# Three products of a delta-rule recurrence in all four quadrants of TensorE, the second head carried across by VectorE, and a weight subtraction moved to GpSimd

## The reference

```python
def delta_rule_scan(r, w, k, v, a, b):          # 12 heads, 512 tokens
    def step(S, inp):
        r_t, w_t, k_t, v_t, a_t, b_t = inp
        sa = jnp.einsum('bhvk,bhk->bhv', S, a_t)
        S = (S * w_t[:, :, None, :] + sa[..., None] * b_t[:, :, None, :]
             + v_t[..., None] * k_t[:, :, None, :])
        return S, jnp.einsum('bhvk,bhk->bhv', S, r_t)
```

## Time and profile before

| | us |
|---|---|
| median of 3 runs (lowest, highest) | 1069.5 (1069.06, 1071.4) |
| profiled execution, its own time | 1070.18 |
| profiled execution, span of its instructions | 1068.4 |
| TensorE busy | 1039.6 |
| VectorE busy | 653.9 |
| ScalarE busy | 453.0 |
| GpSimd busy | 5.6 |

### The profile page before, as it was taken

One profiled execution on the slowest core, in us unless ns is written; L12 is line 12 of the kernel. 1 busy time (PEld: TensorE's weight loads), 2 busy tenths in 40 slices (PEclk: granted clock), 3 DMA queues, 4 the chain that ended last, 5 costly groups with the idle time before them and its releaser, 6 DMA issues.

```text
span 1068.4 us, 22579 instructions
## 1 busy us (share of the span) xinstructions
PE 1039.6 (97%) x9816; PEld 823.4 (77%) x9816; DVE 653.9 (61%) x1025; ACT 453.0 (42%) x732; POOL 5.6 (1%) x10
## 2 busy tenths in 40 slices
PE   7999999999999989999999999999999999999998
PEld 5777777676777777777777767787888888888887
DVE  4569999977466665868677667664443223444322
ACT  5455555686335533443535245344432112443111
POOL 0000000000000000000000000000000000000000
PEclk9999999999999999999999999999999999999999
DMA  9912224000532110110110121322222232223230
GB/s 360 377 61 99 79 81 176 1 2 2 197 118 79 60 42 22 43 42 25 39 42 22 42 81 43 124 93 99 99 99 99 99 99 88 93 96 114 89 104 30
DMA packets 26161, 95.01 MB, mean 89 GB/s; under 512 B 2896, under 2 KB 3152, under 8 KB 25552
## 3 DMA queue, kind: packets, MB, share of 16 engines
q1 hardware_dynamic: 26064, 93.57, 25.1%
HBM read 89.36 MB, written 4.19 MB: 88 GB/s over the span
## 4 chain that ended last, share of the span: by engine, by line
PE 76%; DVE 16%; ACT 4%; issue 2%; DMA 1%; SPq 1%; POOL 0%; ACTq 0%; DVEq 0%
PE psum L857 19%; PE psum L858 18%; PE psum L859 18%; DVE work L2067 5%; PE psum L867 3%; PE psum L1310 2%; PE psum L1323 2%; DVE small_temps L2218 1%; PE psum L1045 1%; PE psum L1024 1%; PE psum L1359 1%; PE psum L1382 1%; DMA work<-weights 1%; DVE in_weights_low L2123 1%; PE psum L1110 1%
## 5 line engine op out<-in xcount | busy, mean ns | idle before, releaser
L2123 DVE TENSOR_TENSOR weights_low<-ring,weights_high 128x1024 fp32r<-128x1024 f32 x70 | 85.8, 1226 | 75.3 <-ACT weights_high L1673 75.3
L1673 ACT ACTIVATE weights_high<-ring 128x1024 fp32r<-128x1024 f32 x70 | 73.6, 1052 | 127.5 <-PE psum L859 127.5
L857 PE MATMUL psum<-normed_high,weights_high 128*128 128x512 f32 x256 | 100.2, 391 | 0.2 <-DVE weights_low L2123 0.2
L859 PE MATMUL psum<-normed_high,weights_low 128*128 128x512 f32 x256 | 99.7, 389 | 0.0
L859 PE MATMUL psum<-hidden_high,weights_low 128*128 128x512 f32 x256 | 99.7, 389 | 0.0
L858 PE MATMUL psum<-normed_low,weights_high 128*128 128x512 f32 x256 | 99.6, 389 | 0.0
L858 PE MATMUL psum<-hidden_low,weights_high 128*128 128x512 f32 x256 | 99.6, 389 | 0.0
L857 PE MATMUL psum<-hidden_high,weights_high 128*128 128x512 f32 x256 | 99.6, 389 | 0.0
L2067 DVE SCALAR_TENSOR_TENSOR work<-work,small_sb 128x512 f32<-128x512 f32 x116 | 80.2, 745 | 0.2
L1643 ACT ACTIVATE work<-psum 128x384 f32<-128x384 f32 (+1 forms) x110 | 54.1, 541 | 56.3 <-PE psum L1359 18.8
L857 PE MATMUL psum<-pair_normed_high,pair_weights_high 128*128 128x512 f32 x176 | 75.8, 431 | 0.8 <-DVE normed_low L2127 0.8
(11 more groups left out here) (320 smaller groups left out, 2102.6 us busy)
## 6 DMA issues: line engine op xcount, KB each, us to landing
ring<-weights SPq DMA_DIRECT2D x135, 512.0 KB, 3.7
work<-weights SPq DMA_DIRECT2D x10, 512.0 KB, 12.9
residual<-xT SPq DMA_DIRECT2D x4, 512.0 KB, 7.1
mixed<-weights SPq DMA_DIRECT2D x4, 512.0 KB, 7.8
residual_saved<-residual SPq DMA_DIRECT2D x8, 256.0 KB, 4.4
residual<-residual_saved SPq DMA_DIRECT2D x1, 2048.0 KB, 9.0
outT<-residual SPq DMA_DIRECT2D x8, 256.0 KB, 3.3
tables_sb<-tables SPq DMA_DIRECT2D x1, 1280.0 KB, 10.4
```

What stands on the lines that cost most here:

```text
L857: pe.matmul(out, wh, high(k), start=first and n == 0, stop=False)
L859: ins = pe.matmul(out, wl, high(k), start=False, stop=last and n == len(order) - 1)
L1673: act.activation(wsplit(q)[0], room_of(b), ACT.Copy).then_inc(w_high, 1)
L2123: vec.tensor_tensor(low, room_of(b), high.bitcast(F32), ALU.subtract).then_inc(w_low, 1)
```

## The change

1. `times_inverse_both` takes the place of the two `times_inverse` at levels 4, 8, 16 and 32 (`CROSSED`; level 2 keeps the old form): for head 1 the output goes to the other half of the rows (`rows(q ^ h)`), so the 16 matmuls of both heads use all four quadrants in turn. It begins when both heads' updates are freed. `masked_values` and `solve` are written the same way; `mv_p` becomes two names, `mv_p_0` and `mv_p_1`, of one bank each.
2. VectorE brings head 1 back to its rows. The mask of head 1 becomes two operations of 64 rows, each read from one half and written to the other; `second_head_values` copies `mv_p_1` in two halves (behind the masks of level 16), and `wu_p_1` is copied in two halves behind level 32. ScalarE copies only head 0's `mv` and `wu`.
3. GpSimd does the 18 `weights_low` of the mixer from `v_0` on, in order, with its two multiplications `KD` behind those of `v_0` and `r_1`; VectorE's `weights_after` are gone. VectorE keeps `wdad`, `gd`, `k_0`, `r_0`, and all from `mix0` on.

```diff
@@ -83,6 +83,7 @@
 MUNITS = 2 * MTILES
+CROSSED = (4, 8, 16, 32)
 MU_AMID, MU_BEHIND = {0: 0, 1: 2, 2: 3, 4: 5}, {0: 1, 3: 4}
@@ -801,12 +802,23 @@
-            for p in range(2):
-
-                pool.wait_ge(bonus_in, p + 1)
-                pool.wait_ge(exps_done, p + 1)
-                k3, l3 = (x.rearrange("p (c t) -> p c t", c=NC) for x in (QW[:], LG))
-                pool.tensor_tensor(KD[p % 2], k3, l3, ALU.mult).then_inc(kd_ready, 1)
+            def weights_low(q):
+
+                b = BLOCK_AT[SPLIT[q]]
+                pool.wait_ge(w_high, q + 1)
+                high, low = wsplit(q)
+                pool.tensor_tensor(low, room_of(b), high.bitcast(F32), ALU.subtract).then_inc(w_low, 1)
+
+            first = SPLIT_AT["v_0"]
+            pool.wait_ge(w_low, first)
+            for q in range(first, SPLIT_AT["mix0"]):
+                weights_low(q)
+                if SPLIT[q] in ("v_0", "r_1"):
+                    p = 0 if q == first else 1
+                    pool.wait_ge(bonus_in, p + 1)
+                    pool.wait_ge(exps_done, p + 1)
+                    k3, l3 = (x.rearrange("p (c t) -> p c t", c=NC) for x in (QW[:], LG))
+                    pool.tensor_tensor(KD[p], k3, l3, ALU.mult).then_inc(kd_ready, 1)
@@ -1302,6 +1314,18 @@
+            def times_inverse_both(p, b):
+
+                names = [f"y{b}_{p}_{h}" for h in range(HEADS)]
+                outs = [take(name, G * C).rearrange("p (c t) -> p c t", c=G) for name in names]
+                for c in range(G):
+                    for q in range(PARITIES):
+                        for h in range(HEADS):
+                            ins = pe.matmul(outs[h][rows(q ^ h), c, :], NT[rows(1 - q), h, c, :],
+                                            XN[rows(1 - q), h, c, :], start=True, stop=True)
+                            if c == G - 1:
+                                full_inc(ins, names[h])
+
             def times_inverse(name, h):
@@ -1342,24 +1366,25 @@
                 pe.wait_ge(*is_free(f"tv_{p}"))
-                out = take(f"mv_{p}").rearrange("p (h c t) -> p h c t", h=HEADS, c=G)
-                for c in range(G):
-                    for h in range(HEADS):
-                        for q in range(PARITIES):
-                            ins = pe.matmul(out[rows(q), h, c, :], MAK[rows(q), h, c, :], TV[rows(q), c, h, :],
-                                            start=True, stop=True)
-                            if (c, h) == (G - 1, HEADS - 1):
-                                full_inc(ins, f"mv_{p}")
-
-            def solve(p, h):
-
-                out = take(f"wu_{p}_{h}").rearrange("p (c n) -> p c n", c=G)
+                outs = [take(f"mv_{p}_{h}", G * C).rearrange("p (c t) -> p c t", c=G) for h in range(HEADS)]
                 for c in range(G):
                     for q in range(PARITIES):
-                        ins = pe.matmul(out[rows(q), c, :], XT[rows(q), h, c, :], TAM[rows(q), c, h, :],
-                                        start=True, stop=True)
-                        if c == G - 1:
-                            full_inc(ins, f"wu_{p}_{h}")
+                        for h in range(HEADS):
+                            ins = pe.matmul(outs[h][rows(q ^ h), c, :], MAK[rows(q), h, c, :], TV[rows(q), c, h, :],
+                                            start=True, stop=True)
+                            if c == G - 1:
+                                full_inc(ins, f"mv_{p}_{h}")
+
+            def solve(p):
+
+                outs = [take(f"wu_{p}_{h}").rearrange("p (c n) -> p c n", c=G) for h in range(HEADS)]
+                for c in range(G):
+                    for q in range(PARITIES):
+                        for h in range(HEADS):
+                            ins = pe.matmul(outs[h][rows(q ^ h), c, :], XT[rows(q), h, c, :], TAM[rows(q), c, h, :],
+                                            start=True, stop=True)
+                            if c == G - 1:
+                                full_inc(ins, f"wu_{p}_{h}")
@@ -1481,9 +1509,9 @@
                     pe.wait_ge(*is_free(f"ta_{p}"))
-                    pe.wait_ge(*is_free(f"mv_{p}"))
+                    pe.wait_ge(*is_free(f"mv_{p}_{h}"))
                     pe.wait_ge(*is_free(f"xf_{p}_{h}"))
-                    solve(p, h)
+                solve(p)
                 if p + 1 < NP:
@@ -1972,8 +2000,8 @@
                     if b == LEVELS[3] and p + 1 < NP:
-                        copy_out(f"mv_{p}", TAM[:, :, :, C:2 * C],
-                                 src=bank(f"mv_{p}").rearrange("p (h c t) -> p c h t", c=G, h=HEADS))
+                        copy_out(f"mv_{p}_0", TAM[:, :, 0, C:2 * C],
+                                 src=bank(f"mv_{p}_0", G * C).rearrange("p (c t) -> p c t", c=G))
                     if p and b == LEVELS[0]:
@@ -2004,8 +2032,7 @@
                     mixed_high(NP - 2)
-                for h in range(HEADS):
-                    copy_out(f"wu_{p}_{h}", WU[:, :, h, :], src=bank(f"wu_{p}_{h}").rearrange("p (c n) -> p c n", c=G))
+                copy_out(f"wu_{p}_0", WU[:, :, 0, :], src=bank(f"wu_{p}_0").rearrange("p (c n) -> p c n", c=G))
                 if p + 2 < NP:
@@ -2276,6 +2303,14 @@
+            def second_head_values(p):
+
+                vec.wait_ge(*is_full(f"mv_{p}_1"))
+                mv = bank(f"mv_{p}_1", G * C).rearrange("p (c t) -> p c t", c=G)
+                for half in range(2):
+                    ins = vec.tensor_copy(TAM[rows(half), :, 1, C:2 * C], mv[rows(1 - half)])
+                free_inc(ins, f"mv_{p}_1")
+
             def invert_pair(u):
@@ -2446,11 +2481,6 @@
-            def weights_after(p, x):
-
-                if group(SPLIT_AT[f"{x}_{p}"] + 2) == 2:
-                    weights_low(SPLIT_AT[f"{x}_{p}"] + 2)
-
             def chunks(x):
@@ -2568,12 +2598,10 @@
                     pair_input(p, x)
-                    weights_after(p, x)
                 changed_key(p)
...
                     pair_input(0, "v")
-                    weights_after(0, "v")
                     bonus(0)
@@ -2603,8 +2631,13 @@
                         vec.wait_ge(*is_full(name))
-                        free_inc(vec.tensor_tensor(Y[:, h], bank(name, G * C).rearrange("p (c t) -> p c t", c=G),
-                                                   mask(f"m{b}", G), ALU.mult), name)
+                        y, m = bank(name, G * C).rearrange("p (c t) -> p c t", c=G), mask(f"m{b}", G)
+                        if h == 0 or b not in CROSSED:
+                            ins = vec.tensor_tensor(Y[:, h], y, m, ALU.mult)
+                        else:
+                            for half in range(2):
+                                ins = vec.tensor_tensor(Y[rows(half), h], y[rows(1 - half)], m[rows(1 - half)], ALU.mult)
+                        free_inc(ins, name)
@@ -2617,6 +2650,8 @@
                         changed_key(late)
+                    if b == LEVELS[3]:
+                        second_head_values(p)
                     if p + 1 < NP:
@@ -2641,7 +2676,6 @@
                         decayed_r(late)
-                        weights_after(late, "r")
                     if norm_late(p - 1):
@@ -2661,14 +2695,19 @@
+                vec.wait_ge(*is_full(f"wu_{p}_1"))
+                wu = bank(f"wu_{p}_1").rearrange("p (c n) -> p c n", c=G)
+                for half in range(2):
+                    ins = vec.tensor_copy(WU[rows(half), :, 1, :], wu[rows(1 - half)])
+                free_inc(ins, f"wu_{p}_1")
                 if p + 1 < NP:
-                    weights_after(p + 1, "v")
                     if norm_late(p - 1):
...
                 else:
+                    vec.wait_ge(w_low, SPLIT_AT["mix0"])
                     for m in range(PAIR_MIX):
@@ -2705,7 +2744,6 @@
                         if n == 5:
-                            weights_after(p + 2, "k")
                             key_squares_rest(p + 2)
```

More of the change, by code:

```diff
@@ L210, in beside_level @@
              4: [f"w_{p + 2}", f"A_{p + 2}"] * (p + 2 < NP)}.get(n, [])
-    behind = {0: [f"gm_{p - 1}"] * (p > 0), 2: [f"mv_{p}"], 3: [f"bon_{p + 1}"], 4: [beside_chain(p, "k")]}.get(n, [])
+    behind = {0: [f"gm_{p - 1}"] * (p > 0), 2: [f"mv_{p}_{h}" for h in range(HEADS)], 3: [f"bon_{p + 1}"], 4: [beside_chain(p, "k")]}.get(n, [])
     return ahead, behind
@@ L339, in psum_order @@
                 if b == LEVELS[2]:
-                    aside(f"mv_{p}")
+                    aside(*(f"mv_{p}_{h}" for h in range(HEADS)))
             o.extend(update)
@@ L1438, in _ @@
                             pe.wait_ge(*is_free(f"x{prev}_{p}_{h}"))
-                        times_inverse(f"y{b}_{p}_{h}", h)
+                        if b not in CROSSED:
+                            times_inverse(f"y{b}_{p}_{h}", h)
+                    if b in CROSSED:
+                        times_inverse_both(p, b)
                     if p == NP - 1:
```

## The result

The changed kernel takes 1088.2 us (median of 4 runs, 1087.2 to 1089.2) against 1069.3 on the same chip: ratio 1.0169, interval 1.0148 to 1.0190, so 18 to 19 us slower. Forecast were +12.6 and 1082.0, with a range up to 1088.0. The likeliest case came, more strongly: the ratio on the forecast's base of 1069.5 gives 1087.6, and the time lies at the upper end of the range.

A forecast was written before the change was run, and what follows sets the result against it. It took TensorE (97% busy) and VectorE as both full in levels 8 to 32. Walk +2.1, `unit_key` stalls +8.0 and pair 0's start +2.5 gave +12.6 us on 1069.5: 1082, 8-in-10 range 1066 to 1088.

The forecast's parts named there:

- The likeliest case: Whole kernel: 12.6 us slower, 1082 us, own range 1074 to 1090, chance 0.65.
- VectorE decides it inside the levels: Levels 8 to 32: both engines full, VectorE with one gap of 0.37 us, so work moved to it decides there.
- A half costs 0.42, not 0.33: VectorE's 64-row mask and value copies: 0.42 us each, as an operation that moves rows may not overlap its neighbour.
- TensorE's 3.5 us a pair: Four level products save 0.55 us each, `masked_values` 0.44, `solve` 0.87: 3.5 us a pair, 21 in six pairs.
- the rival of the missed rate: Products miss the four-quadrant rate because two row halves write one bank: about 5 us on top, 1087 us, chance 0.06.
- GpSimd holds `unit_key`: Behind the v projection, GpSimd's subtraction makes `unit_key` stand 1.6 us in pairs 0 to 4: 8.0 us.
- The sign that I had named: Profile after: `unit_key`, 0.74 us before, takes 2 us or more beside a GpSimd operation of 2.5, in five pairs.
- no stall: Rival: GpSimd does not stall VectorE's two-input operations, only a copy; then +2.1 us, 1071.6 us, chance 0.14.
- The walk, pair 2: Pair 2 followed operation by operation to the chain's first state: 0.9 us longer, 0.1 with low half prices; 0.7 taken.
- Start of pair 0, +1.5: Ahead of pair 0: fewer VectorE subtractions give -1.0 us, but GpSimd's meetings with SBUF work make it about +1.5.
- Pair 5, -0.8: Pair 5, with memory attention between the steps, rests on TensorE more: 0.8 us shorter (-2 to +1).
- The faster rival: VectorE's halves cost less than the TensorE time they free: 1059 to 1066 us, say 1063, chance 0.15.

The follow-up runs named there:

- e11: e3 with each pair of VectorE's half operations made one whole operation, leaving out the exchange of row halves: 1063.6 us, ratio 0.9952.
- e3: Changed kernel with `unit_key` and `bonus_rest` of the next pair moved ahead of the token shift of v: 1080.5 us, ratio 1.0097.
- e7: Changed kernel with the 32 products of `masked_values` done three times in pairs 0 to 4, in TensorE's gap ahead of level 16's product: 1093.6 us.
- e5: e3 with `gn_finish`, `gate`, `decayed_key` ahead of the half copies of `solve`'s second head, and pair 5's two lows ahead of them too: 1073.9 us.
- e12: e8 with only level 4's level product in four quadrants, and VectorE copying one half of `solve`'s second head in pairs 0 to 4: 1064.1 us, ratio 0.9946.
- e6: e2 with `unit_key` and `bonus_rest` moved ahead of the token shift of v: 1069.0 us, ratio 0.9995 to the kernel before.
- e2: Kernel before the change, with only the weight lows moved to GpSimd as in the changed kernel: 1080.9 us, ratio 1.0101.
- e8: e3 with ScalarE instead of VectorE copying the second head of masked values and `solve`, in two halves each: 1069.4 us, ratio 1.0001.

## Why the prediction was right, and where it was off

The direction and the mechanism came as forecast. That the time came so near is in part luck, since errors cancel: of the 18.0 us the holds of `unit_key` are 5.8 by their durations (8.0 forecast), the start is -0.4 (+1.5), the rest of the pairs 0 to 4 is 8.9 (3.9), and pair 5 is +3.7 (-0.8). Two terms came 4.1 lower, two 9.5 higher.

- **VectorE decides it inside the levels**: right. 12.8 us of TensorE's waits at the new product are for VectorE's updates, and without the halves (e11) the kernel is 15 to 17 us faster than e3, pauses included.
- **A half costs 0.42, not 0.33**: right; 64x256 takes 0.422, and two start 0.43 apart. The rule of the Trainium skill, "VectorE: DVE Perf Modes", section "Two Vector instructions with no wait between them", would have it so, and the trace agrees. The copies of 512 are 0.69 each and start 0.70 apart.
- **TensorE's 3.5 us a pair**: a little too much. By groups, a product's busy time fell from 1.16 to 0.72 us, so 0.44 was saved and not 0.55; `solve` saved the forecast 0.87 (1.90 to 1.03). The rate itself was met, so the rival of the missed rate is out: e7's 96 products of `masked_values` take 1.61 us with the 0.22 of the last one, 0.47 for 32. What I had too small was the allowance around them.
- **GpSimd holds `unit_key`**: right in mechanism, place and the number of pairs; the size is 1.15 us (1.90 for 0.74), not 1.6. The meeting came as the walk had it: `unit_key` began 1.01 us into GpSimd's operation, for 0.99. But that operation took 2.36 for the assumed 2.5, and `unit_key` ended 0.55 after it, where the forecast gave it its whole 0.74. 5 x 1.15 = 5.8 for 8.0. The sign that I had named, 2 us or more, was missed by 0.1. So "no stall" is out; it had 0.14. What the rule of the Trainium skill ("SBUF — State Buffer", section "Who interferes with whom") says of two SBUF inputs, the trace agrees with.
- **The walk, pair 2**: `unit_key` starts 0.1 us earlier than before, measured from the pair's start (+0.04 forecast), but before, a pause of 1.17 in TensorE's issue lay ahead of it; in the pairs 1, 3 and 4 it starts 0.3 to 0.4 later. The first state of pair 2 comes 2.7 us later. The walk had 0.9, with the stall 2.5: near, because the stall was 0.45 too large and the walk 0.6 too small (1.5 measured without the stall, 0.9 forecast). Over all five pairs the walk is the term that I made too small, in pair 0 above all: 1.7 without the stall, for 0.3.
- **Start of pair 0, +1.5**: -0.4 to its flipped products. In e3, where the subtractions meet the same SBUF work, the update of level 8 comes 19.8 us behind them, 20.3 before. The gain came: TensorE's 1.22 us of waiting ahead of `turn_pairs` are 0.35. The holds came too: in the changed kernel the copy of 8 elements a row took 2.03 us for 0.16 (from 364.74), and L2621 1.48 for 1.23 (from 384.10). But VectorE rested behind the first, 2.98 us ahead of 377.58, so that it cost next to nothing: the flipped products begin 0.2 us later when counted from 308 us. The +2.5 had priced the holds as if VectorE had no room there.
- **Pair 5, -0.8**: this step failed. I counted the new products as a gain for a pair that "rests on TensorE more", and did not walk VectorE's queue there. The copies wait for `solve`, and what lay beside `solve` for nothing, 2.4 us of lows, falls behind them; with the half copies in the levels it is +3.7. e5 got 2.8 of it back with order alone.
- **The faster rival** (halves cheaper than the TensorE time they free): not here, but its condition holds where the halves go elsewhere. e12 shows that `solve`, `masked_values` and one level product in four quadrants are worth 0.5%, with GpSimd's lows and the moved `unit_key` in it, which alone gave nothing (e6).

Still open: how much of e3's 7.7 us is the stall (5.8 by the durations) and how much the moved work itself, since no run moved it with the subtractions on VectorE. Also open is what places the pauses in TensorE's issue: of those of 0.9 us and more the chain from pair 0 on has one in the kernel before and one in the changed kernel, two in e3, five in e7 and none in e11, so that they blur a comparison of two kernels by a few us. e12 was not run with other sets of levels.

## What to carry to other kernels

When work goes from the busiest engine to one at 61%, read the second engine in the stretch where the work lands: here it had 0.37 us of room, and small operations cost most of their own time. An operation put behind a wait takes all that follows in its queue with it, so walk each queue in each variant of the loop, the last iteration above all. And when GpSimd and VectorE both work on SBUF, what counts is which VectorE operation meets GpSimd's; moving two operations was worth 12 us (e6 against e2).

## What the runs showed of the hardware that was not expected

- A held operation still takes most of its own time once GpSimd's has ended, wherever it met it: `unit_key` began at 501.21 (e2: 499.28) and ended at 503.11 (501.85), 0.55 us after GpSimd's, and so in all ten cases of these two kernels. e11's L2568 began at 493.68 and ended at 494.80, where GpSimd ended at 494.25. The small copy (0.16) ended 0.03 after. So 0.13 to 0.19 us of each had been done while it stood.
- TensorE's clock fell to half in the changed kernel behind idle times of 1.99 us, which did not happen in e2 behind 1.67. With the gap down to 1.05 (e7) it stayed full. The length of the idle time alone does not decide it: pair 0 of the changed kernel has 1.98 and no fall, while the clock fell behind 1.68 in e7 (at 420.34) and in e8 at 399.87, behind 1.35.
- ScalarE's copy from one half of the rows to the other takes 0.59 for 64x512, as 128x512 does (0.60), so two halves cost double there too, as on VectorE; ScalarE only had the room.
